# Attention part of a hybrid GLA, retention and PEER layer: rotary, head norms and level products move to PSUM operands, masks become predicated copies, and scores and transposes move between groups

## The reference, cut to what matters

```python
proj = x @ w_in             # gq, gk (512 each), gv, gr (1024), glr (16), rq, rk, rv, rr (1024 each)
log_a = log_sigmoid(glr @ w_gate_up + b_gate) / 16
o_gla = head_norm(gla_chunk_causal(gq, gk, gv, log_a), gla_g, center=False) * silu(gr)      # 4 heads
o_ret = head_norm(retention(rotary(rq), rotary(rk), rv), ret_g, center=True) * silu(rr)    # 4 heads
h = layer_norm(alpha * x + concat(o_gla, o_ret) @ w_out, ln1_g, ln1_b)
out = layer_norm(alpha * h + peer(h, w_q, subkeys, u_tab, v_tab), ln2_g, ln2_b)            # 16384 experts
```

## Time and profile before

| | us |
|---|---|
| median of three runs | 2140.7 (2140.54 to 2141.9) |
| profiled execution, its own time | 2140.33 |
| its span | 2138.5 |
| TensorE busy | 2074.3 (97%) |
| VectorE / ScalarE / GpSimd busy | 1279.0 / 940.5 / 1120.9 |

### The profile page before, as it was taken

The page is one execution under the profiler, slowest core; times in us unless marked ns, Lnnn a source line. Parts: engine busy times, 40 slices in busy tenths (PEclk is TensorE's granted clock), DMA queues, the critical chain, the costliest instruction groups (busy, mean ns, idle before and its releaser), DMA issues.

```text
span 2138.5 us, 38122 instructions
## 1 busy us (share of the span) xinstructions
PE 2074.3 (97%) x13278; PEld 1882.5 (88%) x13278; DVE 1279.0 (60%) x2005; ACT 940.5 (44%) x1319; POOL 1120.9 (52%) x696
## 2 busy tenths in 40 slices
PE   8999797998999999999999999999999999999997
PEld 8998686788999999999999999988888888888885
DVE  1789206213677786647888888855555555555556
ACT  4544243434444455474444444444444444444442
POOL 6799577686779899988777777710000000000000
PEclk9999899999999999999999999999999999999998
DMA  8556466467767778777666666665555555555553
GB/s 271 147 159 177 131 175 234 143 197 186 173 146 185 185 169 191 179 182 172 158 158 157 157 157 157 158 239 192 185 187 189 183 194 181 194 180 193 181 191 137
DMA packets 148995, 381.32 MB, mean 178 GB/s; under 512 B 15536, under 2 KB 17712, under 8 KB 131136
## 3 DMA queue, kind: packets, MB, share of 16 engines
q1 hardware_dynamic: 148928, 380.40, 62.8%
HBM read 376.15 MB, written 4.19 MB: 178 GB/s over the span
## 4 chain that ended last, share of the span: by engine, by line
PE 78%; POOL 8%; issue 6%; DVE 4%; DVEq 2%; DMA 1%; ACT 1%; POOLq 0%; ACTq 0%; SPq 0%
PE ps L1311 33%; PE ps L1076 13%; PE ps L1077 13%; PE ps L1078 13%; POOL u_lo L1049 5%; POOL w_lo L1025 3%; PE ps L1257 3%; DMA raw<-in_w_in 1%; PE ps L1159 1%; DVE o_sb L771 0%; PE ps L1072 0%; DVE o_sb L773 0%; DVE b_cum L644 0%; PE ps L1175 0%; DVE proj_n L717 0%
## 5 line engine op out<-in xcount | busy, mean ns | idle before, releaser
L1049 POOL TENSOR_TENSOR u_lo<-u_t,u_hi 128x512 fp32r<-128x512 f32 x512 | 669.1, 1332 | 131.7 <-ACT u_hi L518 131.0
L1076 PE MATMUL ps<-xT_hi,u_hi 128*128 128x256 f32 x2048 | 585.5, 286 | 0.5 <-POOL u_lo L1049 0.5
L1077 PE MATMUL ps<-xT_lo,u_hi 128*128 128x256 f32 x2048 | 579.3, 283 | 0.0
L1078 PE MATMUL ps<-xT_hi,u_lo 128*128 128x256 f32 x2048 | 579.2, 283 | 0.0
L1025 POOL TENSOR_TENSOR w_lo<-raw,w_hi 128x1024 fp32r<-128x1024 f32 x176 | 447.0, 2552 | 145.6 <-ACT w_hi L377 145.4
L518 ACT ACTIVATE u_hi<-u_t 128x512 fp32r<-128x512 f32 x512 | 318.2, 631 | 415.2 <-DVE u_t L817 412.6
L817 DVE STREAM_TRANSPOSE u_t<-u_raw 128x512 f32<-128x512 f32 x512 | 350.2, 700 | 151.4 <-DMA u_raw<-in_peer_u 82.3
L1076 PEld LDWEIGHTS ps<-xT_hi,u_hi 128*128 128x128 f32 x2048 | 392.7, 192 | 1.4 <-POOL u_lo L1049 1.1
L1077 PEld LDWEIGHTS ps<-xT_lo,u_hi 128*128 128x128 f32 x2048 | 392.9, 192 | 0.0
L1078 PEld LDWEIGHTS ps<-xT_hi,u_lo 128*128 128x128 f32 x2048 | 392.6, 192 | 0.0
L1030 POOL TENSOR_TENSOR small<-small 128x1 f32<-128x1 f32 (+1 forms) x3 | 1.8, 603 | 731.5 <-DVE small L1010 731.4
(11 more groups left out here) (181 smaller groups left out, 2681.1 us busy)
## 6 DMA issues: line engine op xcount, KB each, us to landing
u_raw<-in_peer_u SPq DMA_DIRECT2D x512, 256.0 KB, 4.8
v_raw<-in_peer_v SPq DMA_DIRECT2D x128, 1024.0 KB, 4.9
raw<-in_w_in SPq DMA_DIRECT2D x112, 512.0 KB, 3.8
raw<-in_w_out SPq DMA_DIRECT2D x32, 512.0 KB, 4.4
raw<-in_w_peer_q SPq DMA_DIRECT2D x128, 128.0 KB, 4.0
x_sb<-in_x SPq DMA_DIRECT2D x4, 512.0 KB, 9.1
x_again<-in_x SPq DMA_DIRECT2D x1, 2048.0 KB, 8.0
h_dram<-o_sb SPq DMA_DIRECT2D x1, 2048.0 KB, 8.4
```

Of the source, the lines that this page charges most:

```text
L1049: pool.tensor_tensor(u_lo[:, r, :], u_t[:, r, :], u_hi[:, r, :].bitcast(F32), ALU.subtract).then_inc(ulo_done, 1)
L1076: pe.matmul(o, lh, rh, start=start, stop=False, skip_group_check=lint)
L1077: pe.matmul(o, lh, rl, start=False, stop=False, skip_group_check=lint)
L1078: return pe.matmul(o, ll, rh, start=False, stop=stop, skip_group_check=lint)
```

## The change

- **Rotation.** `rotate(g)` reads group g from its PSUM banks, multiplies by the cosines in place there and writes only the results to `proj_n`. It runs on VectorE inside the loop over levels (one for each of groups 2, 3, 4) and after it (group 5). ScalarE's four copies go. Groups 4 to 7 of TensorE wait for `rot_done` in the place of `acc_free`.
- **Levels.** ScalarE writes the exponential to PSUM banks 6-7 (`lvl_x`), and VectorE's two products read it there. The mask product and the sum become one `copy_predicated` from PSUM into `a_gla`. Levels 1 to 6 use banks 4-5.
- **Scores later.** The chunk products and level 0 move from before group 3 to after its step 3, and every level moves half a group later. `gla_out` goes before `ret_scores`, which moves from group 7 to after step 5 of group 9; `ret_out(2)` and `(3)` move from before to after step 0 of group 11.
- **Head norms.** Statistics and gain products read PSUM and write `o_sb`; ScalarE's eight copies go. The power is taken twice, for four heads each, on GpSimd after step 1 of groups 10 and 12. The reciprocal root and the swish are applied together, block by block, from the gate group's own banks, and that frees them.
- **Transposes.** Four of the eight transposes of `o_sb` stand between the steps 3 to 7 of group 13, four between the first steps of group 14.

```diff
-        rot_tmp = at("rot_tmp", BIG + 52 * K, [P, 2, 2, T])
+        rot_tmp = at("rot_tmp", BIG + 80 * K, [P, 2, 2, T])
...
+        lvl_x = bank(6, 2)
...
+        def freed(g):
+            return g + 1 if g < A_END - 2 else g + 1 - (A_END - 2)
...
-                    sp.wait_ge(lvl_acc, LEVELS + 1)
+                    sp.wait_ge(lvl_acc, LEVELS)
...
-            sp.wait_ge(mix_done, 4)
+            sp.wait_ge(acc_free, freed(B_END + 1))
...
-                    act.wait_ge(acc_free, 2 + g)
+                    act.wait_ge(acc_free, freed(g + 1))
...
-                act.activation(lvl_e[:], lvl_e[:], ACT.Exp, scale=-1.0).then_inc(lvl_exp, 1)
...
-            def heads_out(g, h):
...
-                    evac_gla(h + 1)
...
-                    evac_ret(h + 1)
+                if l == 0:
+                    act.wait_ge(lvl_free, 1)
+                act.activation(lvl_x, lvl_e[:].rearrange("p h t -> p (h t)"), ACT.Exp, scale=-1.0).then_inc(lvl_exp, 1)
...
-            for g in range(3, A_END + 1):
+            hi_steps(3, range(STEPS))
+            for g in range(4, A_END + 1):
                 hi_steps(g, (0,))
-                if g > 3:
-                    level_exp(2 * g - 7)
-                hi_steps(g, (1, 2, 3))
-                evac_n(g - 1, proj_n, 4 * (g - 1))
-                hi_steps(g, (4,))
-                if g < A_END:
-                    level_exp(2 * g - 6)
+                level_exp(2 * g - 8)
+                hi_steps(g, (1, 2, 3, 4))
+                level_exp(2 * g - 7)
                 hi_steps(g, (5, 6, 7))
             for g in range(A_END + 1, B_END):
-                hi_steps(g, (0,))
-                heads_out(g, 0)
-                hi_steps(g, (1, 2, 3))
+                hi_steps(g, range(4))
                 evac_t(g - 1) if g <= V_END else gate(g - 1)
-                hi_steps(g, (4,))
-                heads_out(g, 2)
-                hi_steps(g, (5, 6, 7))
-            hi_steps(B_END, range(4))
-            act_turn(act, 1, 0)
-            act_turn(act, 1, 1)
+                hi_steps(g, range(4, STEPS))
+            for c in range(3):
+                act_turn(act, 1, c)
+                hi_steps(B_END, (c,))
+            act_turn(act, 1, 3)
             gate(B_END - 1)
-            act_turn(act, 1, 2)
-            later_turns(B_END, 1)
+            for c in range(4, 8):
+                hi_steps(B_END, (c - 1,))
+                act_turn(act, 1, c)
+            hi_steps(B_END, (7,))
             for g in range(B_END + 1, O_END):
                 hi_steps(g, range(STEPS))
...
-                s = bank(6 - 2 * (n % 2), 2).rearrange("p (a b) -> p a b", a=8)
...
                 if n == 0:
-                    dve.tensor_tensor(a8, s, m8, ALU.mult).then_inc(lvl_acc, 1)
+                    dve.tensor_tensor(a8, s, masks[:, LEVELS:LEVELS + 1, :].to_broadcast([P, 8, P]), ALU.mult).then_inc(lvl_free, 1)
                     dve.drain()
                     dve.tensor_copy(a8[0:CH, :, CH:P], bank(4)[0:CH, :].rearrange("p (a b) -> p a b", a=8))
                     dve.tensor_copy(a_far[:].rearrange("p h n -> p (h n)"), bank(5)).then_inc(far_sb, 1)
                 else:
-                    dve.wait_ge(lvl_acc, n)
-                    dve.tensor_tensor(lvl_tmp[:], s, m8, ALU.mult)
                     dve.drain()
-                    dve.tensor_tensor(a8, a8, lvl_tmp[:], ALU.add).then_inc(lvl_acc, 1)
+                    dve.copy_predicated(a8, masks[:, n - 1:n, :].bitcast(U32).to_broadcast([P, 8, P]), s).then_inc(lvl_acc, 1)
...
+            def rotate(g):
+                dve.wait_ge(step_free, used(g))
+                both = bank(2 * (g % 2), 2).rearrange("p (h s t) -> p h s t", h=2, s=2)
+                dst = proj_n[:, 4 * g:4 * g + 4, :].rearrange("p (h s) t -> p h s t", s=2)
+                t1, t2 = both[:, :, 0, :], both[:, :, 1, :]
+                dve.tensor_tensor(rot_tmp[:, :, 0, :], t2, sin2, ALU.mult)
+                dve.tensor_tensor(rot_tmp[:, :, 1, :], t1, sin2, ALU.mult)
+                dve.drain()
+                dve.tensor_tensor(t1, t1, cos2, ALU.mult)
+                dve.tensor_tensor(t2, t2, cos2, ALU.mult)
+                dve.drain()
+                dve.tensor_tensor(dst[:, :, 0, :], t1, rot_tmp[:, :, 0, :], ALU.subtract)
+                dve.tensor_tensor(dst[:, :, 1, :], t2, rot_tmp[:, :, 1, :], ALU.add).then_inc(rot_done, 1)
...
@@ -696,29 +693,43 @@
                 if l:
                     dve.wait_ge(lvl_ready, l)
                 dve.tensor_tensor(blocks(lvl_e), bb, bb[:, :, m - 1:m].to_broadcast([P, GH * T // (2 * m), 2 * m]), ALU.subtract).then_inc(lvl_diff, 1)
+                if l % 2 == 0:
+                    rotate(2 + l // 2)
                 gather(l)
                 dve.wait_ge(lvl_exp, l + 1)
-                dve.tensor_tensor(lvl_q[:], gq, lvl_e[:], ALU.mult)
-                dve.tensor_tensor(lvl_k[:], gk, lvl_e[:], ALU.mult).then_inc(lvl_ready, 1)
...
-            dve.wait_ge(acc_free, 2 + A_END)
...
-            for h in range(0, 2 * RH, 2):
-                t1, t2 = both[:, h:h + 2, 0, :], both[:, h:h + 2, 1, :]
-                dve.tensor_tensor(rot_tmp[:, :, 0, :], t2, sin2, ALU.mult)
-                dve.tensor_tensor(rot_tmp[:, :, 1, :], t1, sin2, ALU.mult)
-                dve.drain()
-                dve.tensor_tensor(t1, t1, cos2, ALU.mult)
-                dve.tensor_tensor(t2, t2, cos2, ALU.mult)
-                dve.drain()
-                dve.tensor_tensor(t1, t1, rot_tmp[:, :, 0, :], ALU.subtract)
-                dve.tensor_tensor(t2, t2, rot_tmp[:, :, 1, :], ALU.add).then_inc(rot_done, 1)
-                dve.drain()
-                if h == 2:
-                    gather(LEVELS)
+                dve.tensor_tensor(lvl_q[:], gq, x4, ALU.mult)
+                dve.tensor_tensor(lvl_k[:], gk, x4, ALU.mult).then_inc(lvl_ready, 1)
+            rotate(A_END - 1)
+            gather(LEVELS)
...
+            def head_stats(h):
+                for a in range(TT):
+                    dve.bn_stats(stat6[:, a * 8 + h, :], both_heads(h % 4)[:, a, :])
+            def head_moments(first):
...
+                    for h in range(first, first + 4):
+                        n = a * 8 + h
+                        dve.bn_aggr(mv[:, n, :], stat6[:, n:n + 1, :])
...
+            dve.wait_ge(gains_in, 32)
+            for h in range(GH):
+                dve.wait_ge(o_mm, h + 1)
+                head_stats(h)
+                c = slice(h * GDV, (h + 1) * GDV)
+                dve.tensor_tensor(o_sb[:, :, c], both_heads(h), gains[:, c].unsqueeze(1).to_broadcast([P, TT, GDV]), ALU.mult).then_inc(o_norm, 1)
+            head_moments(0)
+            v4 = pairs(var16)[:, :, 0:4]
...
+            dve.scalar_tensor_tensor(v4, v4, EPS, mva[:, :, 0:4, 1], ALU.add, ALU.add).then_inc(stat_done, 1)
...
+            def ret_norm():
+                for h in range(RH):
+                    dve.wait_ge(ro_mm, h + 1)
+                    head_stats(4 + h)
+                head_moments(4)
+                dve.tensor_scalar(pairs(var16)[:, :, 4:8], mva[:, :, 4:8, 1], EPS, None, ALU.add).then_inc(stat_done, 1)
+                for h in range(RH):
+                    c = slice(K + h * RDV, K + (h + 1) * RDV)
+                    for a in range(TT):
+                        n = a * 8 + 4 + h
+                        ins = dve.scalar_tensor_tensor(o_sb[:, a, c], both_heads(h)[:, a, :], mv[:, n, 0:1], gains[:, c], ALU.subtract, ALU.mult)
+                    ins.then_inc(ro_norm, 1)
...
+            def mix_block(n):
+                g = V_END + n
+                z = ps[:, 2 * (g % 2):2 * (g % 2) + 2, :]
                 dve.wait_ge(sig_done, n + 1)
-                dve.tensor_tensor(swish[:, :, n * COL:(n + 1) * COL], ps[:, 2 * (g % 2):2 * (g % 2) + 2, :], sig[:], ALU.mult).then_inc(acc_free, 1)
-            def mix_block(n):
-                c = slice(n * COL, (n + 1) * COL)
-                dve.tensor_tensor(o_sb[:, :, c], o_sb[:, :, c], swish[:, :, c], ALU.mult).then_inc(mix_done, 1)
-            for h in range(GH):
...
-            swish_block(V_END)
...
-            dve.tensor_scalar(var16[:], var16[:], EPS, None, ALU.add).then_inc(stat_done, 1)
...
-            for a in range(TT):
-                for h in range(8):
-                    n = a * 8 + h
-                    o = o_sb[:, a, h * GDV:(h + 1) * GDV]
-                    if h < GH:
-                        dve.tensor_scalar(o, o, rstd[:, n:n + 1], None, ALU.mult)
-                    else:
-                        dve.tensor_scalar(o, o, mv[:, n, 0:1], rstd[:, n:n + 1], ALU.subtract, ALU.mult)
...
-                dve.tensor_tensor(o_sb[:, a, :], o_sb[:, a, :], gains[:], ALU.mult)
-            dve.drain()
+                dve.tensor_tensor(z, z, sig[:], ALU.mult)
+                dve.wait_ge(rstd_done, 1 + n // 2)
+                dve.drain()
+                for h in (2 * n, 2 * n + 1):
+                    c = slice(h * GDV, (h + 1) * GDV)
+                    for a in range(TT):
```

(99 more changed lines are left out.)

72 lines of the change are left out of this document (20 added, 52 removed).

## The result

The changed kernel takes 2107.2 us (median of four runs, 2106.3 to 2108.7) against 2141.2 (2140.5 to 2141.9): ratio 0.984, interval 0.983 to 0.985. The forecast was 2105.6, in a range of 2103 to 2112.5.

A forecast was written before the change was run, and what follows sets the result against it. TensorE, busy 97% of the span, was taken as the bound. Stalls -36.1 us, plus 0.5 for switches and 0.5 for group 12's loads, gave -35.1: span 2103.4, median 2105.6 us, range 2103 to 2112.5.

The forecast's parts named there:

- The three stalls as the whole prize: TensorE's idle and slowed time around chunk products, `ret_scores` and group 13: 36.1 us, all that the change can win.
- third: TensorE's stall before group 13, waiting for `swish_block`: loss 17.5 us, 13.9 of it idle, expected to go.
- The clock term: TensorE's products run slower at the lower clock behind the two long stalls: 4.1 us on top of the idle time.
- first stall: TensorE's wait for `decay_done` at the chunk products before group 3: loss 4.1 us (2.7 to 5.2), expected to go.
- Rotation at 0.7 us an instruction: VectorE's six `rotate` instructions with one PSUM operand: 0.69 us each, 4.2 us a round, bounds 4.2 and 17.
- second stall: TensorE's wait at `ret_scores` for the last rotation: loss 14.5 us, 12.9 of it idle, expected to go.
- Levels: VectorE's level work: products 2.4 us, `copy_predicated` 1.2; rotation and gather have 4.7 us before delaying TensorE, so no cost.
- Head norms: Statistics and gain products ready before group 12 wants the banks, with 9 us of cover; the third stall goes.
- Transposes: `o_sb` transposes in groups 13 and 14 cause no wait; 1.1 us counted as won, extra switches cost 0.5 us together.
- Loads of group 12: Later DMAs and a power on GpSimd tighten group 12's loads: 0.5 us put on the path; rival of stopping TensorE 12%.
- what is won is kept: Behind group 14 only semaphore counts change and TensorE bounds both expert phases, so the gain carries to the end.
- The rival on PSUM operands: A PSUM operand spares VectorE nothing: 39.1 us in four level stalls, 47 with low clock, 2152 us; chance 3 in 100.

The follow-up runs named there:

- u1: Changed kernel with the chunk products and level 0 moved back ahead of group 3: median 2111.0 us, ratio 0.986 to the kernel before.
- u2: Changed kernel, but ScalarE copies groups 2 to 5 to SBUF and `rotate` reads the copies: median 2111.2 us, ratio 0.986 to the kernel before.
- u4: Changed kernel, but ScalarE copies the retention heads to SBUF for statistics and gain products: median 2106.4 us, ratio 0.983 to the kernel before.
- u5: Changed kernel with all eight transposes of `o_sb` in and ahead of group 14 as before: median 2108.7 us, ratio 0.985 to the kernel before.
- u3: Changed kernel with levels as before: exponential in SBUF, mask product and sum instead of `copy_predicated`: median 2117.5 us, ratio 0.989 to the kernel before.
- b2: Kernel before, its two long stalls filled with 118 and 128 idle transposes: median 2139.8 us, ratio 0.999.
- b1: Kernel before, its two long stalls filled with 140 and 150 idle transposes: median 2143.0 us, ratio 1.000.
- g3: Changed kernel with each `copy_predicated` of levels 1 to 6 done four times: median 2107.9 us, ratio 0.984 to the kernel before.
- g6: Changed kernel with each `copy_predicated` of levels 1 to 6 done seven times: median 2122.7 us, ratio 0.991 to the kernel before.
- u6: Changed kernel, but the exponential goes to SBUF for the two level products; `copy_predicated` stays: median 2108.4 us, ratio 0.984 to the kernel before.

## Why the prediction was right

- **The three stalls as the whole prize.** Right: 36.1 us priced from starts and clock, 35.6 gained in the stretch after 0.5 us for the wait in group 12. Adding the three waits of the earlier trace rows alone would have said 28.8. Which edit removed which stall is shown for the first alone (u1). For the second and third it is known by elimination: SBUF operands (u2, u4) and the old transposes (u5) don't bring them back, so what is left is the order of the lists, with the banks of group 10 freed block by block. No run put that order back, and none undid u2's and u3's forms together.
- **The clock term.** Right in size, shown by b2 (3.4 of 4.1). For the first stall the low clock stands in three profiles (before, b1, b2), but not in u1, which paid 2.4 us for the stall, not 4.1.
- **Rotation at 0.7 us an instruction.** Right. The upper bound of 17 us was reached in one round of four (16.9, the others 10.5 to 13.1), and in this order all of it would have cost 3.4 us. So the second stall was not won by the cheaper rotations.
- **Levels.** "Cost on the path: nothing" held, with 1.4 us for the unknown instruction. Its cover, put at 4.7 us, is 4.4 at least by g3 and 4.8 by the longest wait of g6. What I did not see is that the PSUM operands and the predicated copy together carry 8.4 us, where the copy alone nearly does (u6). Whether the operands alone would do was not run; g3 speaks for it, since the old gather is at most 3.3 us longer than the copy (an estimate: 1.2 + 3.4 for its two instructions, less 1.4) and 4.4 more were covered.
- **Head norms.** Right, with more cover than claimed (11.2 us and not 9); the PSUM form of the retention heads is worth nothing (u4). The GLA heads' part was not tried alone.
- **Transposes.** Right: 1.3 us in groups 13 and 14 by u5, where 1.1 was counted.
- **Loads of group 12.** Right in place, engine and step, but the size is luck. The account had step 0's low half 2.2 us early and step 2's 1.1 early, and put 0.5 on the path as a margin. It counted the 2.4 us of `ret_out` twice: the start of the DMAs at 2.8 us is reckoned from 316.38, which already has the two heads inside. Without it the slack is 2.8 - 3.0, about nothing; 0.4 us was measured, and then 0.4 + 0.3 + 0.3 - 1.7 is 0.6 late, where 0.5 was measured. The price also varies, 0.1 to 0.9 us over the group's 21.8. One of the signs of being wrong, a wait of TensorE for `w_lo` early in group 12, did appear; the sum had its price in it.
- **The median.** 1.6 us above forecast: 1.1 in the span (2104.5 against 2103.4) and 0.5 since the median lies 0.9 above the profiled execution, not 0.4. The attention stretch won 0.5 more than the sum. The weak term is the base: the sum was made against the span of the one execution whose V phase had no fall of the clock, and "what is won is kept" lost 1.6 us there.
- **The rival on PSUM operands** fell by L679's and L701's durations. Its price looks too high too: it took GpSimd to be working without pause, and u2 and u3, which undo the rotation and the levels one at a time, cost 3.4 and 8.4 us, where it had 39 us of stalls for both.

## What to carry to other kernels

Price a stall of TensorE by the starts on both sides of it, the slower products behind it included: here the table of waits said 28.8 us and the stalls were worth 36.1. An instruction with two SBUF operands beside a busy GpSimd has no one price: here it was 1.2 to 3.4 us for 1024 elements, and less than 1 us of shift upstream went from one end to the other; with one operand in PSUM it stayed at 1.2. But a cheaper instruction is worth what it does at its place: the same slow rotations that stood before a stall of 12.8 us cost 3.4 us once they were spread over the levels. Where a bank must come free, see first whose list stands in front of the instruction that frees it.
